# 32 more tokens of an expert layer served by fetched rows, with half of the one-hot keys built on ScalarE

## The reference, cut to what matters

```
s = einsum('nhid,hikd->nhik', q, sub_keys)          # 8 heads, 2 halves, 128 keys each
s_top, i_top = top_k(s, 16)
cand = s_top[:, :, 0, :, None] + s_top[:, :, 1, None, :]
best, pos = top_k(cand.reshape(n, 8, 256), 16)
idx = i_top[..., 0] * 128 + i_top[..., 1]           # taken at pos
w = softmax(best)
act = gelu(einsum('nhkd,nd->nhk', u_tab[idx], h))
out = einsum('nhk,nhkd->nd', w * act, v_tab[idx])
```

## Time and profile before

| | us |
|---|---|
| median of 3 runs | 3167.16 (3166.33 to 3173.5) |
| profiled execution | 3161.69 |
| its span, first to last instruction | 3159.8 |
| first product | about 1935 to 2592 |
| second product | about 2592 to 3142 |
| TensorE busy in the whole span | 3035.7 (96%) |
| VectorE busy | 2171.6 (69%) |
| ScalarE busy | 1153.0 (36%) |
| moved by DMA | 571.10 MB, mean 181 GB/s |

### The profile page before, as it was taken

One profiled execution on the slowest core, in us unless ns is written; L12 is line 12 of the kernel. 1 busy time (PEld: TensorE's weight loads), 2 busy tenths in 40 slices (PEclk: granted clock), 3 DMA queues, 4 the chain that ended last, 5 costly groups with the idle time before them and its releaser, 6 DMA issues.

```text
span 3159.8 us, 43037 instructions
## 1 busy us (share of the span) xinstructions
PE 3035.7 (96%) x17723; PEld 2789.4 (88%) x17723; DVE 2171.6 (69%) x3782; ACT 1153.0 (36%) x1569; POOL 405.0 (13%) x264
## 2 busy tenths in 40 slices
PE   7998998999999999999999999999999999999998
PEld 7888887888879888988877879999999989999998
DVE  6546975755643443567763468997997858889997
ACT  2234233222233342455553223445444533323322
POOL 0000000000000000000000000011112236655552
PEclk9989998999999998999999999999999999999999
DMA  6223112222232233212223333557778899999996
GB/s 234 109 98 143 43 52 107 76 92 106 78 130 81 73 110 127 79 67 81 72 109 153 125 115 138 192 182 237 254 229 302 299 338 394 393 393 394 392 393 238
DMA packets 215714, 571.10 MB, mean 181 GB/s; under 512 B 14288, under 2 KB 129488, under 8 KB 180064
## 3 DMA queue, kind: packets, MB, share of 16 engines
q1 hardware_dynamic: 176496, 426.14, 37.7%
q0 software_dynamic: 36864, 134.23, 11.4%
q10 hardware_dynamic: 2160, 7.99, 0.7%
HBM read 495.95 MB, written 72.35 MB: 180 GB/s over the span
## 4 chain that ended last, share of the span: by engine, by line
PE 69%; DVE 16%; DMA 10%; ACT 3%; issue 1%; SPq 1%; DVEq 0%; ACTq 0%
PE bank L580 61%; DMA wv<-weight_spill 8%; DVE wl L535 4%; PE bank L1243 2%; DVE acc L149 2%; PE bank L644 2%; PE bank L2514 1%; PE bank L592 1%; DVE ub L3274 1%; PE bank L651 1%; DVE pl L3217 1%; DVE Ah L3050 1%; PE bank L2523 1%; DMA gelu_spill<-gst 1%; DVE gv L3206 1%
## 5 line engine op out<-in xcount | busy, mean ns | idle before, releaser
L580 PE MATMUL bank<-hh,wh 128*128 128x512 f32 (+2 forms) x2512 | 909.8, 362 | 19.6 <-DVE wl L535 9.2
L580 PE MATMUL bank<-hl,wh 128*128 128x512 f32 (+2 forms) x2512 | 881.7, 351 | 0.0
L580 PE MATMUL bank<-hh,wl 128*128 128x512 f32 (+2 forms) x2512 | 881.4, 351 | 0.0
L528 ACT ACTIVATE wh<-ring 128x2048 fp32r<-128x2048 f32 (+2 forms) x249 | 463.8, 1863 | 778.8 <-PE bank L580 755.2
L535 DVE TENSOR_TENSOR wl<-ring,wh 128x2048 fp32r<-128x2048 f32 (+2 forms) x249 | 554.3, 2226 | 281.1 <-ACT wh L528 276.8
L580 PEld LDWEIGHTS bank<-hh,wh 128*128 128x128 f32 x2512 | 479.2, 191 | 69.8 <-issue 18.0
L580 PEld LDWEIGHTS bank<-hl,wh 128*128 128x128 f32 x2512 | 479.0, 191 | 45.9 <-issue 6.0
L580 PEld LDWEIGHTS bank<-hh,wl 128*128 128x128 f32 x2512 | 477.7, 190 | 42.6
L580 PE MATMUL bank<-ph,wh 128*128 128x384 f32 x1024 | 346.9, 339 | 24.4 <-DVE pl L3217 17.8
L3260 POOL DMA_INDIRECT ub<-in_urow,gsel x112 | 175.4, 1566 | 1381.4 <-DVE gsel L2977 870.8
L580 PE MATMUL bank<-ph,wl 128*128 128x384 f32 x1024 | 344.6, 337 | 0.0
(11 more groups left out here) (520 smaller groups left out, 4451.8 us busy)
## 6 DMA issues: line engine op xcount, KB each, us to landing
ring<-in_v SPq DMA_DIRECT2D x68, 1024.0 KB
ring<-in_u SPq DMA_DIRECT2D x64, 1024.0 KB
ring<-in_ada SPq DMA_DIRECT2D x24, 1024.0 KB
gelu_spill<-gst SPq DMA_DIRECT2D x128, 192.0 KB
weight_spill<-stage SPq DMA_DIRECT2D x24, 1024.0 KB, 11.5
gv<-gelu_spill SPq DMA_DIRECT2D x64, 384.0 KB
wv<-weight_spill SPq DMA_DIRECT2D x64, 384.0 KB
ring<-in_wup SPq DMA_DIRECT2D x22, 1024.0 KB
```

The lines of the kernel that those rows point to most:

```text
L528: a.then_inc(a.e.activation(wh[q % 2][:, 0:n], ring[k % 4][:, 0:n], ACT.Copy), s("whi"))
L580: ins = p.e.matmul(out, l, r, start=start and i == 0, stop=stop and i == len(pairs) - 1, skip_group_check=not check)
```

## The change

The dense products are computed for 352 tokens instead of 384. The tokens 128 to 159 (`GX` = 32) join the fetched ones. Their 128 choices are laid out as four groups of 32 on the partitions (partition 32a + i holds token i's choices 32a to 32a+31), so that 32 additional fetches of 128 rows serve them for `u` and 32 for `v`: 320 fetches instead of 256. Their h is transposed by 16 short matmuls in the third weave and copied to the four groups of partitions by DMA; their sums are held in `accx` and folded over the four groups by a matmul with `fold`. The schedule is changed: `ROWS = 0, 32, 64, 124, 148`, so 148 fetches are consumed under the first product and 172 in the second, and `CHOOSE` = 1.42. There are 88 quads instead of 96. Of a quad's four `Ah` columns VectorE now writes two; ScalarE writes the other two as relu(w - w (key - x)^2), with one Square and one Relu each (`first_keys_sc`). The copy from PSUM to `stage` is written in runs of four elements. The last weight block holds 32 tokens and has a DRAM tensor of its own, `last_weight_spill`, whose rows on a partition are 256 bytes.

```diff
+GX = 32
+ND = 512 - GT - GX
+NQ = ND // 4
+NU = 128 + GX
+TAILS = ND - 320
...
     def quads(j):
-        return [(32 * j + q - 32, q) for q in range(32)]
+        return [(32 * j + q - 32 - GX // 4, q) for q in range(GX // 4 if j == 1 else 0, 32)]
...
+    def first_keys_sc(a, t, q):
+        if t >= 2:
+            a.wait_ge(s("ab_mm"), t - 1)
+        for z in (2, 3):
+            k = 4 * q + z
+            ins = a.e.activation(Ah[t % 2][:, z, :], C["iota"], ACT.Square, scale=-1.0, bias=ijw[:, 0, k:k + 1])
+        a.then_inc(ins, s("sc"))
+        a.settle()
+        for z in (2, 3):
+            k = 4 * q + z
+            ins = a.e.activation(Ah[t % 2][:, z, :], Ah[t % 2][:, z, :], ACT.Relu, scale=nw[:, k:k + 1],
+                                 bias=ijw[:, 2, k:k + 1])
+        a.then_inc(ins, s("ah"))
...
     def hot_sc(a, j):
+        a.wait_ge(s("ijw"), j)
+        first_keys_sc(a, *quads(j)[0])
         for t, q in quads(j):
+            if q < 31:
+                first_keys_sc(a, t + 1, q + 1)
             a.wait_ge(s("ab_mm"), t + 1)
-            a.then_inc(a.e.activation(place[:, :, 4 * (q % 16):4 * (q % 16) + 4].rearrange("p j t -> p t j"),
-                                      quad(bank[5 + t % 3][:, :]), ACT.Copy), s("stg"))
+            a.then_inc(a.e.activation(place[:, :, 4 * (t % 16):4 * (t % 16) + 4],
+                                      quad(bank[5 + t % 3][:, :]).rearrange("p t j -> p j t"), ACT.Copy), s("stg"))
...
     def hot_ve(v, j):
-            for z in range(4):
+            for z in range(2):
...
     def hot_sy(y, j):
-        for z in range(4):
-            yield
-            if j > 1:
-                spill(y, 2 * j - 3, z)
-        for q in range(32):
-            yield
-            if q in (16, 18, 20, 22):
-                spill(y, 2 * j - 2, (q - 16) // 2)
+        for t, q in quads(j):
+            yield
+            if t >= 16 and t % 16 in (0, 2, 4, 6):
+                spill(y, t // 16 - 1, t % 16 // 2)
...
-    ROWS = 0, 16, 32, 64, 68
+    ROWS = 0, 32, 64, 124, 148
...
-        yield from weave((hot(1), 1), (top(2), 0.75), (rows(ROWS[0], ROWS[1]), 0.4))
-        yield from weave((hot(2), 1), (top(3), 0.75), (rows(ROWS[1], ROWS[2]), 0.4))
-        yield from weave((hot(3), 1), (rows(ROWS[2], ROWS[3]), 0.8))
+        yield from weave((hot(1), 1), (top(2), 0.93), (rows(ROWS[0], ROWS[1]), 1.07))
+        yield from weave((hot(2), 1), (top(3), 0.75), (rows(ROWS[1], ROWS[2]), 0.84))
+        yield from weave((hot(3), 1), (rows(ROWS[2], ROWS[3]), 1.58))
...
-    CHOOSE = 1.14
+    CHOOSE = 1.42
...
+        y.e.dma_start(wv5[i % 3][:, :, :], wl_[i]).then_inc(s(f"gv{i % 3}").sem, 16)
     def weigh(v, i):
-        g4 = gv[i % 3][:, :, :].rearrange("p x (b t) -> p x b t", b=6)
-        for x in range(2):
-            ins = v.e.tensor_tensor(g4[:, x], g4[:, x], wv[i % 3][:, :, x, :], M)
+        g4 = gv[i % 3][:, :, 0:320].rearrange("p x (b t) -> p x b t", b=5)
+        v.e.tensor_tensor(g4, g4, wv[i % 3][:, :, :, :].rearrange("p b x t -> p x b t"), M)
+        g5 = gv[i % 3][:, :, 320:ND]
+        v.then_inc(v.e.tensor_tensor(g5, g5, wv5[i % 3][:, :, :], M), s("gw"))
...
     def gather_po(g):
-        for n in range(256):
+        for n in range(2 * NU):
+            if n == 128:
+                g.wait_ge(s("gx"), 16 * (128 // GX))
...
     def v_pe(p):
-                    ins = mm3(p, vbank[d][:, GT:512], ...)
+                    ins = mm3(p, vbank[d][:, GT + GX:512], ...)
```

More of the change, by code:

```diff
@@ L468, in _build @@
     dot = flat(mT[:, :, :])
+    gsent = cst[:, past + 400:past + 656].rearrange("p (c k) -> p c k", c=2)
+    gx = cst[:, past + 656:past + 656 + 2 * GX].bitcast(U32).rearrange("p (c k) -> p c k", c=2)
+    dotx, gwtx, fold = [hhu[:, k, 528:528 + GX] for k in range(3)]
+    hTx = cst[:, CONST["lvl0"][0]:CONST["lvl0"][0] + 1024].rearrange("p (k n) -> p k n", k=8)
+    accx = hlu[:, :, 16 + GT:16 + GT + 128]
     by_h8 = lambda ap: ap.rearrange("p (h k) -> p h k", h=8)
     spare = hlu[:, :, 16:16 + GT]
-    ijw = spare[:, 0:3, :]
+    ijw, nw = spare[:, 0:3, :], spare[:, 7, :]
     paf = [spare[:, 3 + c, 0:64].bitcast(B16) for c in range(2)]
@@ L3016, in hot_pe @@
             p.then_inc(ins, s("ab_mm"))
+            if j == 3 and q in (4, 8):
+                x = q // 4 - 1
+                p.wait_ge(s("ijw"), 3)
+                if x:
+                    p.wait_ge(s("hx"), 1)
+                for k in range(4 * x, 4 * x + 4):
+                    for n_, h_ in enumerate((hh, hl)):
+                        ins = p.e.matmul(bank[4][0:GX, 128 * (k % 4):128 * (k % 4) + 128],
+                                         h_[:, k, 16 + GT:16 + GT + GX].bitcast(F32), ident,
+                                         start=k % 4 == 0 and n_ == 0, stop=True, skip_group_check=True)
+                p.then_inc(ins, s("hx_mm"))
             yield
         yield
+    def first_keys_sc(a, t, q):
[11 more added lines that the diff above has]
+        a.then_inc(ins, s("ah"))
     def hot_sc(a, j):
@@ L3025, in hot_sc @@
             a.wait_ge(s("ssp1"), 16)
+        a.wait_ge(s("ijw"), j)
+        first_keys_sc(a, *quads(j)[0])
         for t, q in quads(j):
-            b, place = t // 16, stage[t // 16 % 2]
+            b, place = t // 16, stage[t // 16 % 2][:, :, :]
+            if b == 5:
+                place = flat(place)[:, 0:128 * TAILS].rearrange("p (j t) -> p j t", t=TAILS)
+            if q < 31:
+                first_keys_sc(a, t + 1, q + 1)
             if b >= 2:
@@ L3030, in hot_sc @@
             a.wait_ge(s("ab_mm"), t + 1)
-            a.then_inc(a.e.activation(place[:, :, 4 * (q % 16):4 * (q % 16) + 4].rearrange("p j t -> p t j"),
-                                      quad(bank[5 + t % 3][:, :]), ACT.Copy), s("stg"))
+            a.then_inc(a.e.activation(place[:, :, 4 * (t % 16):4 * (t % 16) + 4],
+                                      quad(bank[5 + t % 3][:, :]).rearrange("p t j -> p j t"), ACT.Copy), s("stg"))
+            if j == 3 and q in (5, 9):
+                x = q // 4 - 1
+                a.wait_ge(s("hx_mm"), x + 1)
+                a.wait_ge(s("seld"), 8)
+                a.then_inc(a.e.activation(hTx[0:GX, 4 * x:4 * x + 4, :], quad(bank[4][0:GX, :]), ACT.Copy), s("hx"))
             yield
@@ L3040, in hot_ve @@
         if j >= 2:
-            v.wait_ge(s("ab"), 32 * j - 32)
+            v.wait_ge(s("ab"), quads(j)[0][0])
+            v.wait_ge(s("ah"), quads(j)[0][0])
+        ts(v.e, nw, bank[4][:, 256:384], -1.0, M)
         v.then_inc(v.e.tensor_copy(ijw, bank[4][:, 0:384].rearrange("p (c k) -> p c k", c=3)), s("ijw"))
@@ L3288, in gather_sc @@
     def gather_sc(a, i):
-        for b in range(4):
-            if 32 * b + 31 in GATHER_AT[i - 2] or i == 2 and 32 * b + 31 < RU:
-                c = slice(32 * b, 32 * b + 32)
-                a.wait_ge(s("gd"), 32 * b + 32)
+        for b in range(5):
+            end = 32 * b + 32 if b < 4 else NU
+            if end - 1 in GATHER_AT[i - 2] or i == 2 and end <= RU:
+                to, of = (gwt[:, 32 * b:32 * b + 32], dot[:, 32 * b:32 * b + 32]) if b < 4 else (gwtx, dotx)
+                a.wait_ge(s("gd"), end)
@@ L3293, in gather_sc @@
                 a.wait_ge(s("wst1"), WST[1])
[L3294 removed]
+                a.then_inc(a.e.activation(to, of, ACT.Gelu_apprx_tanh), s("gg"))
     def start_idle():
@@ L3361, in v_ve @@
     def v_ve(v):
+        v.then_inc(v.e.tensor_reduce(fold, ident.rearrange("p (a c) -> p c a", c=GX), AX.X, A_), s("fold"))
         for i in range(64):
```

94 lines of the change are left out of this document (62 added, 32 removed).

## The result

| | us |
|---|---|
| before, median of 5 runs of the comparison | 3167.16 (3159.55 to 3173.79) |
| after, median of 5 runs | 3187.44 (3183.08 to 3198.99) |
| ratio after / before | 1.0061, 95% interval 1.0042 to 1.0079 |
| span of the profiled execution | 3185.6 (before 3159.8) |

The change makes the kernel 0.6% slower, about 20 us, where I had forecast 24 us less.

A forecast was written before the change was run, and what follows sets the result against it. TensorE was taken to bound the first product, TensorE and DMA bytes both the second. Terms -36 + 0 - 2 (last tiles at TensorE's pace) + 6 + 8 = -24 us gave a median of 3143 us, range 3118 to 3178.

The forecast's parts named there:

- -36 us at the end of the third weave: First product, searches through third weave: the larger of VectorE's and TensorE's needs plus small losses, 587 us against 623.
- term (b): ScalarE's keys in the weaves: in-order stalls now reach TensorE; +8 us, bounds 0 and 25.
- From there on it is bytes: After the third weave, DMA bytes at 394 GB/s set the time: 230 MB before, 229 MB after.
- 0 us: After the third weave: bytes saved by narrower tiles are eaten by the 64 additional fetches, so no change.
- the 10 us that I had set beside the sum: Tail of 256-byte packets in the wv tile: 10 us more if each costs as much as 512 bytes.
- Term (a): Behind the third weave: fetch 124 waits for weight block 4 to land, VectorE stands; +6 us, bounds 0 and 15.
- Tables: ScalarE's Squares and Relus in each quad: no activation table loads beside Gelu's, 0 us.
- Rival 3: Rows 0 to 63: fetches through two buffers too slow, +70 us whole, 30 half-way; 3173 to 3210 us, chance 0.16.
- Rival 2: Nothing is won: ScalarE's in-order stalls or 256-byte packets take the 24 us back; 3170 us, chance 0.19.
- The two signs by which I said I would be wrong: TensorE waiting over 20 us in sum for Ah in the weaves, or VectorE waiting for ub before 2400.

The follow-up runs named there:

- e11: Changed kernel with VectorE multiplying only the first 8 of 128 columns per block of each fetched u row; 3158.58 us (before: 3167.59).
- e9: Changed kernel loading only 16 of 2048 columns of each u tile from the fifth tile on; 3160.18 us (before: 3167.59).
- e12: Changed kernel with the edits of e9 and e11 together; 3144.20 us (before: 3167.59).
- e4: Changed kernel without the 64 additional fetches, tokens 128 to 159 getting no expert output; 3151.22 us (before: 3169.66).
- e14: e13 with the edits of e9 and e11 added; 3127.03 us (before: 3170.35).
- e8: e4 with all Ah columns (keys) back on VectorE; 3136.72 us (before: 3171.76).
- e13: Changed kernel: gelu spill on ScalarE's queue, keys one quad earlier, second product's first loads later, gated fetch 12 rows later; 3171.55 us, ratio 1.0008 to before.
- e5: Changed kernel with ScalarE's keys written one quad earlier; 3189.12 us, ratio 1.0069 to before.
- e2: Changed kernel with the gelu (product) spill issued from ScalarE's DMA queue instead of SP's; 3175.18 us, ratio 1.0019 to before.

## Why the prediction was wrong

**The step that failed: "-36 us at the end of the third weave".** Counted as the prediction counts, from phase to phase up to the last `Bh`:

| | before | forecast change | after | change |
|---|---|---|---|---|
| turn and searches | 91 | -9 | 90 | -1 |
| first weave | 186 | -29 | 165 | -21 |
| second weave | 185 | -12 | 187 | +3 |
| third weave | 128 | +14 | 153 | +24 |
| sum (before rounding) | 590 | -36 | 596 | +6 |

42 us are missing, 8 to 15 in each phase; 8 of them my term (b) had provided for. They are not in the work: the distance of 352-column matmuls is 0.159 us (forecast 0.160), and VectorE is busy for the time forecast in the first two weaves and for less in the third. They are in the losses that I had added to the larger of two needs: 14 and 12 us in the first two weaves, 4 in the searches and 5 in the third weave. VectorE and TensorE feed each other through two buffers of `wl` and two of `Ah`/`Bh`, and each now waits for a third party too: VectorE for fetched rows (27.6 us ahead of 2562 where it had 2.5), TensorE for ScalarE's half of the keys (26.0). Some part is the clock, which I hadn't costed at all: ahead of the cut about 15 us in matmuls at the long distance, 2 before. What each is worth in the weaves' part: row work 28 us (e11), `u`'s bytes 18 (e9), both together 34 (e12), the additional rows in all 23 (e4).

That the needs of the two engines lie so close together is not by itself the cause. Two stretches of the second weave of the changed kernel, the dense search and behind it:

```profile
2210.00:2260.00 50.00, 43.61 (x274) 43.16 (x273) 45.44 (x144) 31.45 (x65) 10.46 (x8) 0.93 0.64 220
2300.00:2350.00 50.00, 50.00 (x331) 50.00 (x330) 47.62 (x110) 34.45 (x67) 14.96 (x11) 1.00 0.80 261
```

Behind the search TensorE is busy for all of the 50 us with VectorE at 95%; in the search both fall short, at 87 and 91%. And the count of TensorE's own matmuls shows how much the experiments leave open. Taking its `u` matmuls at their full-clock distance (0.1735 us before, 0.1593 after) and 0.89 us a quad, the weaves' part divides so:

| | weaves' part | TensorE's own matmuls | the rest |
|---|---|---|---|
| before | 590 | 569 | 21 |
| after | 596 | 500 | 96 |
| e9 `u` not loaded | 578 | 501 | 77 |
| e11 short row multiplies | 568 | 500 | 68 |
| e12 both | 562 | 499 | 63 |
| e14 both, and the order | 562 | 515 | 47 |
| e4 no additional rows | 573 | 521 | 52 |
| e8 the same, keys on VectorE | 569 | 521 | 48 |

The rest (waits, the clock, some 5 us of transposes) grew by 75 us. Row work and `u`'s bytes take 33 of them away, the changes of order in e14 another 16. About 30 us are there even without the additional rows, in e4 with VectorE at 85% or less in every weave and in e8 with no keys on ScalarE; for them no run has a cause.

**What was right.** "From there on it is bytes" holds in every kernel here, at 384 GB/s for the 394 that I took. The *0 us* was off by the count: 233.1 MB for 228.5, +12 us. Behind the cut the trace has 200 fetches for 193 before, where my list had 196 for 192, and 27.8 MB of weights where it had 25.2. The second product itself is 508 us for 537, -29, below the 517 to 530 I named, but what it gained was paid in the 40 us by which the stretch from the last `Bh` to the last gelu grew (59 to 99). The packets of 256 bytes are too few to show in the rate: 384 GB/s with them as without. But in the packets' own records behind the cut 16384 of them take 19 ns each, where the ones of 512 bytes take 28: a third more for their bytes, 4.6 us of 16 engines, about half of the 10 us that I had set beside the sum. The Trainium skill ("DMA: Bandwidth & Descriptors", Specifications) has transfers under 512 B below the full rate; this trace agrees in the direction, at 19 ns for 28.

**Term (a), +6 for the gate.** The wait is there, 12.6 us, and VectorE then stands 8.7 us for the first row behind it. What it costs isn't shown: e13 left 9.1 us of it and gained about 2. That in a stretch bound by bytes such a wait isn't added to the bytes is the likelier reading. **Term (b), +8 for ScalarE in order.** ScalarE's keys do hold TensorE for 26 us, but e5 shows that writing them earlier moves the wait to `wl`, and e8 beside e4 that they cost only 3 us without the rows. The wait is where the weave's slack runs out, and not a term to add. Its prices were off both ways: a quad's keys take 1.5 us for the 1.1 to 1.3 forecast, the copy into `stage` 0.58 for 1.1, and ScalarE is busy 61% of the second weave and of the third, not 80 to 84. What of ScalarE's part makes it, the settle between Square and Relu or the order behind copy and split, no run has separated. **Tables: 0**, as forecast: at lines 3052 and 3057 the Squares take 0.39 us each and the Relus 0.49, with no load beside them.

**The rivals.** Rival 3, the two buffers of rows 0 to 63, is in part what happened: VectorE waits for fetches ahead of 2392 as well (24.8 us, 11.3 of them in the second weave), though its 30 to 70 us did not come. Rival 2's cause, ScalarE's stalls, makes half of TensorE's waits (26.0 us) and not in the third weave alone, but by e5 and e8 it isn't what costs. The two signs by which I said I would be wrong both came: over 20 us of waits for `Ah`, and VectorE waiting for `ub` ahead of 2400. None of the rivals had a loss in every phase, of short waits and the clock that falls behind them.

**What stays open.** By the count above the clock takes some 13 us more ahead of the cut and the standing 44, but which of these would go with the other isn't settled, as every run that shortened the waits much raised the clock with them. The cause of about 30 us of the rest isn't either. And 8 us of the difference of the two profiled spans lie in a part that the change doesn't touch.

## What to carry to other kernels

When two engines that feed each other through two buffers both come near to filling the stretch, and one of them waits for fetches too, don't add a small loss to the larger need: here the weaves with needs of 148 against 143 us and 162 against 161 took 165 and 187, 12 and 16% more, where with 178 against 162 they had taken 186, 4% more. Work that is moved from a lone, cheap, regular producer (matmul columns) to a chain over four engines and a full DMA queue must be priced by that chain: the 64 fetches cost 42 us where the narrower products saved 24. And once a part runs at the DMA ceiling, count its bytes first, to the row: all sixteen programs moved 379 to 387 GB/s there, and e2, which cut ScalarE's waits for spills around its start from 62.9 to 8.0 us, made it 5 us shorter.

## What the runs showed of the hardware that I had not expected

A wait of TensorE of 4.5 us was followed by 5 us at 0.54 of the clock, matmuls of 352 columns 0.293 us apart for 0.159; the time in such stretches rose from 13.7 to 78.5 us of the first product as the waits rose. With the queues near full, two DMA issues of 32 KB held SP's queue for 6.63 and 6.51 us where the same issue a moment earlier took 0.56. Packets of 256 bytes took 19 ns each, those of 512 bytes 28. And the same 176 KB spills, issued from ScalarE's queue instead of SP's with its 1 MB loads, cut ScalarE's waits for them from 110.0 to 18.3 us.
